# Attention in a hybrid encoder block: where TensorE turns the outputs of a head's last query block

## The reference

```python
def chunk_causal_attention(q, k, v):
    ...
    def one_block(args):
        qi, qc = args
        sc = jnp.einsum('bhqd,bhkd->bhqk', qi, k).astype(jnp.float32) * scale
        mask = key_chunk[None, :] <= qc[:, None]
        sc = jnp.where(mask, sc, -jnp.inf)
        p = jax.nn.softmax(sc, axis=-1).astype(v.dtype)
        return jnp.einsum('bhqk,bhkd->bhqd', p, v)
```

## Time and profile before

| | us |
|---|---|
| median of 3 runs | 2318.3 (2317.56 to 2318.71) |
| the profiled execution | 2320.36 |
| its span, first to last instruction | 2318.6 |
| mean granted TensorE clock | 0.978 |
| PE busy | 2196.4 (95%) |
| DVE busy | 1052.3 (45%) |
| ACT busy | 902.9 (39%) |

### The profile page before, as it was taken

One profiled execution on the slowest core, in us unless ns is written; L12 is line 12 of the kernel. 1 busy time (PEld: TensorE's weight loads), 2 busy tenths in 40 slices (PEclk: granted clock), 3 DMA queues, 4 the chain that ended last, 5 costly groups with the idle time before them and its releaser, 6 DMA issues. The chain is left out here.

```text
span 2318.6 us, 32826 instructions
## 1 busy us (share of the span) xinstructions
PE 2196.4 (95%) x11569; PEld 1819.4 (78%) x11569; DVE 1052.3 (45%) x1875; ACT 902.9 (39%) x1676; POOL 342.5 (15%) x326
## 2 busy tenths in 40 slices
PE   7999999999989999999978989999999998999998
PEld 6888887778868888888866767777888877778886
DVE  6111000100014555544446666777777766564652
ACT  7212111100113444433433335556656665443441
POOL 1221214032201111111111420000000022000000
PEclk9999999999989999999989999999999999999999
DMA  5222122231312323333266863333312336573751
GB/s 187 82 70 77 59 80 73 84 112 59 113 49 78 95 91 99 95 100 95 82 207 217 288 187 77 73 71 71 67 37 48 73 100 199 176 229 126 207 155 64
DMA packets 215332, 257.99 MB, mean 111 GB/s; under 512 B 37713, under 2 KB 136465, under 8 KB 212753
## 3 DMA queue, kind: packets, MB, share of 16 engines
q1 hardware_dynamic: 186000, 203.59, 30.7%
q10 hardware_dynamic: 23552, 42.50, 4.9%
q0 software_dynamic: 5696, 10.79, 1.7%
HBM read 159.28 MB, written 97.54 MB: 111 GB/s over the span
## 5 line engine op out<-in xcount | busy, mean ns | idle before, releaser
L74 PE MATMUL bankD<-hT_hi,shared_w_hi 128*128 128x512 f32 x512 | 212.5, 415 | 7.2 <-POOLq L881 7.2
L76 PE MATMUL bankD<-hT_hi,shared_w_lo 128*128 128x512 f32 x512 | 202.1, 395 | 0.0
L75 PE MATMUL bankD<-hT_lo,shared_w_hi 128*128 128x512 f32 x512 | 201.3, 393 | 0.0
L74 PE MATMUL bankA<-hT_hi,shared_w_hi 128*128 128x512 f32 x512 | 200.7, 392 | 0.0
L76 PE MATMUL bankA<-hT_hi,shared_w_lo 128*128 128x512 f32 x512 | 199.6, 390 | 0.0
L1859 DVE TENSOR_REDUCE small_chunk_min<-scores 128x1 f32<-128x512 f32 (+2 forms) x320 | 181.9, 606 | 38.9 <-PE scores L76 25.2
L75 PE MATMUL bankA<-hT_lo,shared_w_hi 128*128 128x512 f32 x512 | 199.4, 390 | 0.0
L1879 ACT ACTIVATE probs<-scores,small_least 128x1024 f32<-128x1024 f32 (+2 forms) x192 | 167.3, 871 | 12.8 <-DVE small_least L1866 11.6
L74 PE MATMUL bankA<-wt_hi,hT_hi 128*128 128x512 f32 x384 | 150.1, 391 | 4.5 <-DVE shared_v_raw L498 2.5
L2013 DVE TENSOR_TENSOR pT<-turn_rest,pT 128x512 fp32r<-128x512 f32 (+2 forms) x208 | 126.2, 625 | 54.5 <-ACT pT L1979 54.5
L75 PE MATMUL bankA<-wt_lo,hT_hi 128*128 128x512 f32 x384 | 149.4, 389 | 0.0
(11 more groups left out here) (269 smaller groups left out, 4664.9 us busy)
## 6 DMA issues: line engine op xcount, KB each, us to landing
shared_w_raw<-in_w_in_dram SPq DMA_DIRECT2D x32, 512.0 KB, 4.5
projT<-stage ACTq DMA_DIRECT2D x64, 256.0 KB, 2.4
projT<-d_stage ACTq DMA_DIRECT2D x64, 256.0 KB, 2.4
e_l_in<-projT SPq DMA_DIRECT2D x64, 256.0 KB, 5.0
gateTok<-stage ACTq DMA_DIRECT2D x32, 256.0 KB, 2.0
shared_w_lo<-hgTok SPq DMA_DIRECT2D x16, 512.0 KB, 3.4
knT<-b_out SPq DMA_DIRECT2D x32, 256.0 KB, 3.6
vTok<-b_out SPq DMA_DIRECT2D x32, 256.0 KB, 4.3
```

Source lines behind the costliest of these rows:

```text
L74: pe.matmul(out, a_hi, b_hi, start=first, stop=False)
L75: pe.matmul(out, a_hi, b_lo, start=False, stop=False)
L76: return pe.matmul(out, a_lo, b_hi, start=False, stop=last)
```

## The change

TensorE no longer turns the output of a head's last block at the end of that head. It does so in step 0 of the next head, after score row 9 and ahead of the transposes. The wait for its end and the count for `head_done` move with it. The three other blocks of each head, and block 3 of the last head, stay where they were. The programs of ACT, DVE and SP are unchanged.

```diff
+            def turn_output(h, o_block):
+                at = TURN_AT["o", o_block]
+                pe.wait_ge(o_copied, h * NB + (o_block + 2))
+                pe.wait_ge(turn_read, h * TURNS + (at - 1))
+                for r in range(TPB):
+                    last = pe.matmul(turn[at % TURN_RING][:, r * VD:(r + 1) * VD], oT[:, r * P:(r + 1) * P], fold[:], start=r == 0,
+                                     stop=r == TPB - 1, skip_group_check=True)
+                last.then_inc(turned, 1)
+                if o_block == NB - 1:
+                    pe.wait_ge(turned, h * TURNS + TURNS)
+                    pe.sem_inc(head_done, 1)
...
                         queries(pe, h + 1, i, 1 - u)
+                    if step == 0 and h > 0:
+                        turn_output(h - 1, NB - 1)
                     for tile in before:
...
-                    if o_block is not None:
-                        at = TURN_AT["o", o_block]
...
-                        if o_block == NB - 1:
-                            pe.wait_ge(turned, h * TURNS + TURNS)
-                            pe.sem_inc(head_done, 1)
+                    if o_block is not None and (o_block < NB - 1 or not more):
+                        turn_output(h, o_block)
```

## The result

The changed kernel takes 2326.13 us (median of 18 runs, 2321.34 to 2335.22) against 2318.17 us before (18 runs, 2311.08 to 2324.15). The ratio is 1.0035, with a 95% interval of 1.0025 to 1.0046: slower by 8 us, where 8.5 us faster was forecast. The profiled execution took 2322.12 us with a span of 2320.3, the third shortest of the 18.

The account below looks back on a forecast made before the run. PE's order of work and waits were taken to set the attention; 7 x 1.7 = 11.9 us saved, less 0.8 for loads and 2.6 for two clock drops, gave 8.5 saved: 2309.8 us, range 2306.8 to 2316.8.

Parts of the forecast that it names:

- Step 1: PE at a seam: row 9 starts right after the values, and the later turn needs no wait for `oT`.
- Step 2: Behind the turn: DVE's scaling of the output, hidden before, is now bare; PE idles 0.65 us.
- Step 3: DVE's minima follow the last output; tile (0, 3)'s transpose, the mark, comes 1.7 us earlier per seam, PE idling 1.45.
- Rival E: DVE's chain is longer than worked out: each 0.25 us per seam costs 1.8 in all; no chance of its own.
- Step 4: At full clock the reordering alone gains 0.1 us per seam; the other 1.6 need the slow stretch gone.
- Step 5: PE's clock behind seams: drops at 2 of 7 (bounds 0 and 7), 1.3 us each, on row 10 and the values.
- Rival B: Clock drops at 5 to 7 seams: 2313.7 us with 5, 2316.3 with 7; chance 0.22.
- rival D: Slower: the slow stretch at a seam lasts twice as long, 3.0 us per seam, 2328 us; chance 0.06.
- Step 6: Loads behind `head_done` come 2.6 us later against the head's work; ACT's wait for head 7's branch weights costs 0.8, once.
- Rival C: Turns and transposes count for nothing to the clock: a full 1.7 us drop at every seam, 2319.1 us; chance 0.07.

Follow-up runs that it names:

- experiment 1: Changed kernel with DVE's loop over heads written out: 2313.52 us, 0.9972 of the kernel before.
- experiment 3: Changed kernel with seven unused filler matmuls per seam on PE behind the turn, ahead of tile (0, 3): 2314.98 us, 0.9983 of the kernel before.
- experiment 4: Kernel before with three unused filler matmuls on PE ahead of the turn of a head's last output: 2310.97 us, 0.9963 of the kernel before.
- experiment 8: Kernel before with filler matmuls ahead of the turn and DVE's loop over heads written out: 2309.22 us, 0.9950 of the kernel before.
- experiment 2: Changed kernel with DVE's loop written out and row 9's minima taken ahead of scaling the last output: 2309.83 us, 0.9961 of the kernel before.
- experiment 6: Changed kernel with the turn after row 9's first chunk and DVE's loop written out: 2303.49 us, 0.9927 of the kernel before.
- experiment 9: Kernel before with the turn moved only at the seam between heads 3 and 4: 2317.50 us, 0.9998 of the kernel before.
- experiment 14: Kernel before, nothing changed, the third of three repeated profiles: 2312.43 us.
- experiment 5: Changed kernel with the turn after row 9's first chunk instead of after all of it: 2307.15 us, 0.9952 of the kernel before.

## Why the prediction was wrong

**Step 1, row 9 and the turn: right.** Row 9 follows the values by 0.11 and nothing holds it. The turn needs no wait. It was issued 1.96 after the last matmul of values; forecast was 1.94.

**Step 2, the bare scaling: right.** PE idles 0.57 behind the turn (forecast 0.65).

**Step 3, DVE's chain: failed by one term.** It had the minima begin 0.1 us after `o_out` ends. The measured gap is 0.78, the turnround of DVE's loop over heads, which experiment 1 took away (0.21). In the timeline of before that gap lies under the wait for row 9's scores, and nothing in the earlier trace rows tells it from that wait; the position of the loop in the code does. It made the mark 1.0 earlier instead of 1.7 and PE's idle time 2.07 instead of 1.45. Rival E named a longer chain, with 0.9 us per seam as the point from which it loses the verdict. That holds only if no seam has a drop: from the forecast's own 8.5 us, with its 2 drops, the point is (8.5 - 4.6) / 7 = 0.56. The 0.7 was past it even before it touched the clock.

**Step 4, the order by itself: right that it is worth little, wrong in sign.** Forecast was 0.1 us gained per seam at full clock. Experiments 3 and 4 measured 0.5 lost, which is this 0.1 less the 0.7 of step 3. Experiments 1 and 8 measured 0.05 gained with the loop out of the way.

**Step 5, the clock: the step that lost the forecast.** It had drops at 2 of 7 seams at 1.3 us. The price was right for a plain one (1.3, experiment 3 against the changed kernel). The count was not: 21 of 21 in three profiles, five of them long at 2.5 to 2.9. Rival B had the drops (5 to 7) and a reason for them, rival D their doubling, each alone; what happened is B with D at some seams. The seam was placed between the earlier trace rows. With 2.07 us of idle time it was on the bad side of them. Experiment 1, with 1.36, has 6 of 7 seams clean, experiments 2 and 6, with 0.95, all of them. But the idle time does not decide alone. The seventh seam of the changed kernel idles 1.54, near the 1.45 forecast, and has its drop in all three profiles, and in experiment 9 a seam lost its drop by what happened one seam earlier. How many drops the forecast's own 1.45 would have brought was not measured.

**What the sum was made against.** The one profile of before had drops at all 7 seams and I took that for the kernel. Three more have 7, 4 and 3. A seam of before without a drop gives a head of 66.7, and none of the changed kernel's did. So 11.9 us could never be saved against the median: the changed kernel pays 0.5 at a seam without a drop, 0.3 or more with a plain one, and has drops where before often had none.

**Step 6, the loads: direction right.** In the changed kernel ACT waited 0.17 us for the weights in head 7; forecast 0.8. But the forecast was for shorter heads. With the clock at 1.00 the wait was 1.90 in the new order (experiment 3) against none in the old (experiment 4); with the loop written out as well it was 1.06 (experiment 1) against 1.19 (experiment 8), so the moved count is not all that it depends on. What it costs the kernel was not measured.

**The terms together, an estimate from these figures.** Between 8.5 us saved and 8 us lost lie 16.5. The turnround gives 6 x 0.7 + 0.2 = 4.4, five more drops 5 x 1.3 = 6.5, the long ones (five in three profiles, some 1.4 more each) 2.3, and the attention of before, 468.8 on average instead of 472.4, gives 3.6. The loads take 0.6 off. That is 16.2, good to about 2, for instance because the drop at the seventh seam costs under 1.3.

**Rival C, that turns and transposes do not count for the clock.** The drops at every seam are what it asks for. The third repeated profile of before (experiment 14) speaks against it. Behind the last matmul of values, from 1921.24 to 1929.02, PE has only 32 transposes, one turn and 3.25 us of idle time. Windows over that stretch and the next:

```profile
1921.10:1929.00 7.90, 4.68 (x42) 4.33 (x40) 5.29 (x9) 4.62 (x9) 0.00 (x0) 1.00 0.50 126
1929.00:1935.80 6.80, 6.78 (x30) 5.65 (x31) 0.87 (x2) 1.06 (x1) 0.00 (x0) 1.00 0.99 304
```

The clock is 1.00 in both. If turns and transposes were as good as idle, this would be 7.8 us of idling. From the turn to the mark of the changed kernel, where the clock fell 21 times of 21, it is 4.9. In other profiles the clock did fall at the end of this stretch, as in the earlier trace rows, but the rival asks for that every time. Experiments 1, 2 and 6 fit with that, but do not settle it, since they shorten the whole stretch with the idle time in it. How much transposes count against other matmuls was not measured. The Trainium skill, "TensorE: Matmul & The Clock Gate", section "Part 4: PE-mode transpose", says of transpose mode that "it doesn't count as PE-busy the same way". It speaks of transposes alone, and the trace records those of this kernel as MATMUL like the rest; by that rule the clock should have fallen behind the stretch above, and this profile does not agree.

**A reading that was off without harm.** The clock line in the earlier trace rows has two slices at 8, not one.

## What to carry to other kernels

Moving a stalled instruction behind other work pays only if what its result releases has cover in the new place: list what each other engine does between the moved instruction and the next point at which the first engine waits, the turnround of its loops included. A profile of one execution shows one way in which the clock fell. Where a period's time depends on it, read several profiles before pricing a gain from it: here the four of one kernel had 7, 4, 7 and 3 drops. Where a row of work can be divided, put the stalled step inside it, with one part ahead to cover its input and the rest behind to cover its consumers: here that turned 8 us lost into 13 us won (experiment 5), or 16 with DVE's loop written out (experiment 6).

## What the runs showed of the hardware

A slow stretch of 3.4 us costs 1.3 us in the changed kernel (68.62 against 67.30), since part of it falls on idle PE. Matmuls of no use, 1.86 us of them in 2.07 us of idle time, took the changed kernel from 1.0035 to 0.9983 of before, as they kept the clock at 1.00. In experiment 9 the slow stretches coupled neighbouring seams: one seam that was 1.5 us longer was followed by an unchanged one that was 1.5 us shorter. In the kernel before the clock fell at seams with no longer wait of PE ahead of it than 0.77 us, and in experiment 14 it stayed at 1.00 behind a stretch of 7.8 us in which PE had only transposes, a turn and 3.25 us of idle time. The turnround of DVE's loop took 0.74 to 0.78 us in seams that go round the loop and 0.39 in the last, where the loop is left; with the loop written out the gap is 0.21.
